# Moving casts, loads and a small reduction at the seam between the decode and the merge stage

## The reference

```
h = rmsnorm(x, g_pre)
z = h @ w_in           # q_lat, kv_lat, k_r, z_att, u_pool, z_pool, g_att, g_pool
...
o_lat = mla_attend(q_abs, q_r, pos, ckv, kr, k_pos)      # prompt: causal blocks; sample: paged cache
o = einsum('bshr,rhv->bshv', o_lat, w_uv)
y_att = (o * silu(z_att)) @ w_o_att
p, pool_state = pool_mixer(u_pool, pool_hist, pos, w_pool, pool_scale)   # windowed means over 2, 4, 8, 16 tokens
y_pool = (p * silu(z_pool)) @ w_o_pool
merged = sigmoid(g_att) * y_att + sigmoid(g_pool) * y_pool
x = x + merged @ w_out                                   # then rmsnorm(x, g_final)
```

## Time and profile before

| | |
|---|---|
| median of 3 runs | 2125.49 us (2124.41 to 2127.14) |
| profiled execution, its own time | 2128.32 us |
| its span, first to last instruction | 2126.5 us (1.8 us lie around it) |
| TensorE busy, matmuls | 2085.4 us, 98% |
| VectorE, ScalarE, GpSimd busy | 1277.5, 972.7, 352.4 us |
| granted TensorE clock, mean | 0.994 of full speed |

### The profile page before, as it was taken

One profiled execution on the slowest core, in us unless ns is written; L12 is line 12 of the kernel. 1 busy time (PEld: TensorE's weight loads), 2 busy tenths in 40 slices (PEclk: granted clock), 3 DMA queues, 4 the chain that ended last, 5 costly groups with the idle time before them and its releaser, 6 DMA issues.

```text
span 2126.5 us, 31437 instructions
## 1 busy us (share of the span) xinstructions
PE 2085.4 (98%) x11893; PEld 1953.7 (92%) x11893; DVE 1277.5 (60%) x2689; ACT 972.7 (46%) x1729; POOL 352.4 (17%) x499
## 2 busy tenths in 40 slices
PE   6999999999999999999999999999999999999997
PEld 6998888888888887799999999999999999999997
DVE  7785878778878775465344644456444644446434
ACT  4445766555555555453334423343334433344333
POOL 3443311011100201150004200050002300041000
PEclk9999999999999999999999999999999999999999
DMA  8876321111110204445434453434534453433532
GB/s 303 251 232 184 92 58 38 45 31 31 31 31 16 100 30 155 152 133 168 136 123 128 141 183 113 145 118 144 165 107 153 131 182 116 128 117 120 178 119 73
DMA packets 159557, 260.44 MB, mean 122 GB/s; under 512 B 21323, under 2 KB 109779, under 8 KB 158247
## 3 DMA queue, kind: packets, MB, share of 16 engines
q1 hardware_dynamic: 153470, 237.59, 35.7%
q0 software_dynamic: 2304, 12.58, 1.6%
q10 hardware_dynamic: 3632, 8.28, 1.3%
HBM read 216.97 MB, written 41.66 MB: 122 GB/s over the span
## 4 chain that ended last, share of the span: by engine, by line
PE 56%; DVE 1%; DMA 0%; ACT 0%; issue 0%; ACTq 0%; POOLq 0%; POOL 0%; DVEq 0%
PE b_ps L122 56%; PE b_ps L2100 1%; DMA d_ws<-in_w 0%; DVE d_y L1988 0%; ACT d_wr L1241 0%; DVE d_y L2008 0%; DVE d_wr L84 0%; DVE d_y L1990 0%; ACT d_y L1889 0%; POOLq L1619 0%; ACT d_zs L1882 0%; ACTq L1619 0%; ACT d_zs L1865 0%; DVE d_gate_p L2016 0%; DVE d_pool L84 0%
## 5 line engine op out<-in xcount | busy, mean ns | idle before, releaser
L122 PE MATMUL b_ps<-d_ht,d_wr 128*128 128x412 f32 x3840 | 734.8, 349 | 1.0 <-DVE d_wr L84 0.7
L122 PEld LDWEIGHTS b_ps<-d_ht,d_wr 128*128 128x128 f32 x3840 | 715.8, 188 | 5.1 <-issue 1.8
L84 DVE TENSOR_TENSOR d_wr<-d_ws,d_wr 128x1024 fp32r<-128x1024 f32 x260 | 321.3, 1236 | 550.7 <-ACT d_wr L1241 550.7
L1241 ACT ACTIVATE d_wr<-d_ws 128x1024 fp32r<-128x1024 f32 x260 | 275.1, 1058 | 600.6 <-PE b_ps L122 591.7
L746 PE MATMUL b_ps<-kt,k_qs 128*128 128x512 f32 (+2 forms) x1520 | 337.3, 370 | 1.6 <-DVE b_p L1090 1.5
L746 PEld LDWEIGHTS b_ps<-kt,k_qs 128*128 128x128 f32 x1520 | 265.7, 188 | 47.5 <-DVE b_p L1090 2.4
L84 DVE TENSOR_TENSOR b_pt<-b_ps,b_pt 128x512 fp32r<-128x512 f32 x272 | 183.5, 689 | 95.4 <-ACT b_pt L1044 93.5
L1044 ACT ACTIVATE b_pt<-b_ps 128x512 fp32r<-128x512 f32 x272 | 158.7, 597 | 174.0 <-PE b_ps L1150 115.3
L1150 PE MATMUL b_ps<-b_pt,kv 128*128 128x512 f32 x816 | 229.6, 410 | 3.6 <-DVE b_pt L84 3.6
L1037 ACT ACTIVATE b_p<-b_p,b_bias 128x1024 f32<-128x1024 f32 (+7 forms) x192 | 171.5, 896 | 54.4 <-DVE b_low L1097 53.4
L122 PE MATMUL b_ps<-d_mrg,d_wr 128*128 128x412 f32 x960 | 189.8, 353 | 0.0
(11 more groups left out here) (212 smaller groups left out, 2066.0 us busy)
## 6 DMA issues: line engine op xcount, KB each, us to landing
d_ws<-in_w SPq DMA_DIRECT2D x260, 512.0 KB, 3.6
out_q<-a_qout SPq DMA_DIRECT2D x32, 384.0 KB, 4.7
d_hf<-out_ht SPq DMA_DIRECT2D x20, 412.0 KB, 3.5
d_olf<-out_olat SPq DMA_DIRECT2D x40, 206.0 KB, 2.9
a_xt<-in_x_t SPq DMA_DIRECT2D x16, 512.0 KB, 5.2
out_ht<-a_hf SPq DMA_DIRECT2D x16, 512.0 KB, 3.7
out_olat<-b_ol SPq DMA_DIRECT2D x32, 256.0 KB, 4.2
out_y<-d_y SPq DMA_DIRECT2D x5, 1536.0 KB
```

Of the source, the lines that this page charges most:

```text
L84: return e.tensor_tensor(low, source, high.bitcast(f32), ALU.subtract)
L122: mm = pe.matmul(out, stationary(a, k), moving(b, k), start=first and k == 0 and a + b == 0, stop=last and k == depth - 1 and a == 1)
L1241: act.activation(ahead["wr"][k % 2][:, 0, :, :], ahead["ws"][k % 4][:, :, :], ACT.Copy).then_inc(ahead["w_hi"], 1)
```

## The change

Four moves. In decode, ScalarE casts the third quarter of the tokens before the first exponentials, not after them. In merge, SyncE issues the loads of weight tiles 4 and 5 ahead of all its other loads; `pscale` and `gfin` are issued from GpSimd's queue, after its clearing of `y`, and no longer from ScalarE's; VectorE reduces the history after tile 1's preparation of weights, not after tile 0's.

```
             for n in range(STEPS):
                 for j in range(QUAD):
                     keys(n, j)
-                    if n == CHUNKS and j == QUAD - 1:
-                        exponents(0)
                 if n in AHEAD_H:
                     h_high(act, ahead, AHEAD_H.index(n) // 2, AHEAD_H.index(n))
+                if n == CHUNKS:
+                    exponents(0)
...
+            for k in range(2):
+                sp.wait_ge(w_ok, k + 1)
+                load_weights(sp, io, ahead, k + 4)
             load_pick(0)
...
-                    if c < NC - 1 or k + 4 < NW:
+                    if (c > 0 or k >= 2) and (c < NC - 1 or k + 4 < NW):
                         after(sp, (w_ok, NW * c + k + 1))
                         load_weights(sp, io, ahead, k + 4)
...
-            act.dma_start(pscale[:, :], io["pool_scale"]).then_inc(const_in, 16)
-            act.dma_start(gfin[:, :], io["g_final"].partition_broadcast(P)).then_inc(const_in, 16)
...
             pool.memset(last[:, :, :], 0.0).then_inc(head_ok, 1)
+            pool.dma_start(pscale[:, :], io["pool_scale"]).then_inc(const_in, 16)
+            pool.dma_start(gfin[:, :], io["g_final"].partition_broadcast(P)).then_inc(const_in, 16)
...
-                    if c == 0 and k == 0:
+                    if c == 0 and k == 1:
                         history()
```

## The result

The changed kernel takes 2128.86 us (median of 20 runs), the kernel before 2125.41 us (20 runs beside them). The ratio is 1.0016, with a 95% interval of 1.0010 to 1.0022: 3.4 us slower, 2.1 to 4.7, and above the range of the prediction. Two executions of the kernel before were far slower (2157.2 and 3301.83 us) and are not in the ratio; its other 18 lie between 2122.61 and 2130.15, wider than the 0.13% of the first three. The profiled execution took 2128.82 us, its span is 2126.9. The two spans differ by only 0.4 us, because decode begins 4.1 us earlier in the second one (827.00 instead of 831.07 us), for reasons outside the change: in every trace but the one of before it begins between 824.5 and 828.1. So I compare stage by stage, from decode's first issue (`c_own`), from merge's first issue, and to the first ZA tile.

A forecast was written before the change was run, and what follows sets the result against it. It took TensorE, busy 98% of the span, as the bound, with 3.3 us idle where the change acts. Decode's -0.6 and merge's +0.8 gave +0.2 on a median of 2125.5: 2125.7 us, range 2123.4 to 2127.7.

The forecast's parts named there:

- Moved cast: In decode: the earlier cast brings VectorE's subtraction, TensorE's turn and the scores forward; 0.6 us gained, bounds +1.4 and -0.4.
- when `wuv_f` lands: At merge's start: behind the loads of tiles 4 and 5, `wuv_f` lands 1.4 us late, between 0.7 and 2.4.
- Who pays: In merge: the lateness passes through ScalarE's square and GpSimd's line to the first ZA tile; 0.8 us lost.
- Edits costed at nothing: In merge: later history and constants on GpSimd's queue stay covered by GpSimd's wait for the square; no cost.
- rival (b): In merge: GpSimd's own issues of the constants decide from 2.2 us each; at 3.5 us each, 2128.3 us; chance 0.08.
- Rival (a): In merge: GpSimd's line is not the end, `wuv_f` landing nearly as before; about 1.3 us gained, 2124.2; chance 0.20.
- Rival (c): In decode: the token quarter lands 0.6 us or more later, nothing gained there; 2126.3 us or a little more; chance 0.14.
- Rival (d): In merge: tile 4's VectorE subtraction waits behind GpSimd's addition for the port; only 0.7 us gained, 2124.8; chance 0.10.
- The sum: Whole kernel: decode's -0.6 us and merge's +0.8 us give +0.2 us, 2125.7 us; chance 0.48.

The follow-up runs named there:

- e5: Changed kernel with `pick`, `wpl_f` and `wuv_f` issued ahead of tiles 4 and 5, which still precede the latents and the history's copy; 2123.45 us, one run.
- e7: Changed kernel with GpSimd's clearing of `y` and the constants' loads behind it held back until `wpl_f` and `wuv_f` have landed; 2133.43 us, one run.
- e8: Changed kernel with `wuv_f` and `wpl_f` split one tile later and TensorE's wait for the split moved to the first pooling product; 2126.74 us, ratio 1.0010.
- e2: Kernel before with only the loads of tiles 4 and 5 issued ahead of SyncE's other loads; 2128.99 us, ratio 1.0016.
- e9: e5 with the history reduced after tile 0 again, as in the kernel before; 2123.42 us, ratio 0.9992.
- e6: Changed kernel with the loads of tiles 4 and 5 issued in decode, behind the second chunk's token quarters; 2124.26 us, ratio 0.9994.
- e1: Kernel before with only the cast of the third token quarter moved ahead of the exponentials; 2125.09 us, ratio 1.0001.
- e3: Changed kernel with SyncE's order of loads put back; moved cast, constants on GpSimd's queue and later history stay; 2123.97 us, ratio 0.9997.
- e11: Changed kernel with `hist` and `head` issued by SyncE behind `wuv_f`, not by ScalarE; 2130.32 us, one run.
- e12: As the changed kernel, but only tile 4's load goes ahead of SyncE's other loads, tile 5's back in its place; 2125.57 us, ratio 1.0001.

## Why the prediction was wrong

**Moved cast: right.** 0.6 was forecast, about 1.0 measured (58.0 to 58.1 against 59.0 to 59.1). Each step came as written: ScalarE's wait for the landing, the cast, the subtraction 0.9 earlier, the copies after the exponentials as the new end. Only the end was 0.35 too late in my sum: four copies take 2.04 in a row, and the scores follow 0.05 later.

**The step that failed: when `wuv_f` lands.** I took 1.4 us late, with bounds of 0.7 to 2.4; it was 5.5. Both of my bounds count the bytes ahead of `wuv_f`, and the near one takes the rate of decode's burst (1848 KB in 7.25 us). Two things differ here. First, merge starts slower than a burst in decode. Windows of the kernel before from the issue of two weight tiles and two token quarters at 870.59, its second to fourth us, and of the changed kernel from merge's start, the same three and the two after them:

```profile
871.59:872.59 1.00, 1.00 (x20) 0.59 (x16) 0.64 (x1) 0.33 (x1) 0.00 (x0) 1.00 0.87 164
872.59:873.59 1.00, 1.00 (x17) 0.61 (x7) 1.00 (x2) 0.00 (x0) 0.00 (x0) 1.00 1.05 410
873.59:874.59 1.00, 1.00 (x12) 1.00 (x11) 0.42 (x5) 0.92 (x2) 0.00 (x0) 1.00 0.98 389
...
886.05:887.05 1.00, 1.00 (x8) 1.00 (x7) 0.00 (x0) 1.00 (x2) 1.00 (x1) 1.00 1.12 86
887.05:888.05 1.00, 1.00 (x7) 0.99 (x6) 0.87 (x1) 0.42 (x2) 1.00 (x1) 1.00 0.75 154
888.05:889.05 1.00, 1.00 (x7) 1.00 (x6) 0.35 (x1) 0.00 (x0) 1.00 (x3) 1.00 0.79 268
889.05:890.05 1.00, 1.00 (x7) 1.00 (x6) 0.00 (x0) 0.18 (x1) 0.93 (x3) 1.00 0.97 388
890.05:891.05 1.00, 1.00 (x7) 1.00 (x6) 0.02 (x1) 0.88 (x1) 0.65 (x1) 1.00 1.02 385
```

In four microseconds (with the first, 4 GB/s in both) decode moves 967 KB, merge 512 KB: 1.2 us at full rate. (The kernel before starts merge no faster, with 391 KB.) This alone would have stayed within my bounds. By 893.05, 8.0 us after merge's start, 2060 KB had moved (the windows' GB/s times us, with 388 and 384 GB/s for the next two), about the 1800 KB and ScalarE's 270 that I had counted for 7.3 to 9.0 us. Second, and this is what failed, `wuv_f` does not end with these bytes. The queues from merge's start to its landing, in the changed kernel (885.05 to 897.17, the first three rows) and in e5 (885.16 to 891.87, the other two): packets, MB, share of 16 engines; q1 is SyncE's, q0 GpSimd's, q10 ScalarE's:

```profile
q1 hardware_dynamic: 1035, 2.58, 70.2%
q0 software_dynamic: 176, 0.53, 12.3%
q10 hardware_dynamic: 288, 0.28, 6.8%
...
q1 hardware_dynamic: 547, 1.25, 66.0%
q10 hardware_dynamic: 288, 0.28, 13.4%
```

SyncE's 1800 KB up to `wuv_f` are 1.84 MB, so 0.74 MB that it issued behind `wuv_f` had moved as well, and all of GpSimd's `gfin`. That is 1.27 MB more than I counted. At the 329 GB/s of the last four microseconds it takes 3.9 us, nearly the way from 8.0 to 12.1. This is accounting after the fact: why `wuv_f` ended behind these bytes no run shows. Nor is it a rule for every load: in e5 only 0.46 MB from behind `wuv_f` (776 KB with what stands ahead, 0.79 MB) had moved, and nothing of `gfin`. For `gfin` it agrees with what I had weighed from the Trainium skill (DMA: Bandwidth & Descriptors, Issuing engines are not separate DMA queues): DMAs of different queues share the same engines and interleave. I applied it to ScalarE's 270 KB only (at the burst's rate 1.06 us, not the 0.7 I wrote), and not to GpSimd's `gfin`; e7, with `gfin` out of the way, landed 2.1 earlier. What SyncE issues behind `wuv_f` on its own queue I did not count at all.

**Who pays: right in kind.** Put 5.5 where the prediction has 1.4. ScalarE's square and GpSimd's norm are then 5.5 late: 9.82 + 5.51 = 15.33 us after merge's start, and 15.33 is what the trace has (900.38). Less the wait of 0.25, GpSimd would end 5.26 later and the ZA tile come at 33.56 + 5.26 + 0.14 = 38.96. GpSimd's operations took 0.53 more than that (it ended at 924.40, after 39.35), and the tile came at 39.64, because TensorE itself was later still: the text said the hole at tile 4 stays closed only under 1.4 of lateness, and at 5.5 it is open by 3.8. What I had no term for is the clock behind such a hole (1.55 us) and the 0.90 at the pooling product. Two paths of nearly equal length were late, and e8, which cuts one, shows the other: 3.39 at the ZA tile.

**Edits costed at nothing.** An issue on GpSimd's queue costs 0.59 and 0.56, near the low end of my bounds; rival (b) is out. The history a step later was covered by the wait for the square in the change (5.51), and with `hist` late it takes a wait off tile 3 (1.03 in e2). As soon as `wuv_f` is in time it is on GpSimd's path: e5 waited 0.75 at the ZA tile, e9 not. Rival (a) needed `wuv_f` as before and did not occur. Rival (c) is out. Rival (d) did not occur at tile 4: VectorE's subtraction started first, at 901.26, and took 1.24, and GpSimd's addition of 901.32 took 1.92 instead of 0.89. It did occur at the pooling operand, where the subtraction of 918.10 took 1.38 instead of 0.57, most of the 0.90 more wait. The Trainium skill (SBUF — State Buffer, Who interferes with whom) has a VectorE instruction with two SBUF inputs contend with a GpSimd instruction that reads SBUF, and both rows agree.

**The sum.** With the measured sizes, -1.0 + 4.9 gives +3.9, and 3.4 was measured (2.1 to 4.7). That it comes so close is in part luck, since it leaves out the clock and the pooling product. The range failed, because both of its bounds stood on the bytes ahead of one load.

## What to carry to other kernels

Where loads are put in another order at the start of a stage, ask for each one that moves back who waits for it first, and price its landing between the end of what stands ahead of it in its own queue and the end of all that every queue issues in that stretch: here 6.4 to 8.0 us where small loads or none stood ahead, 10.0 to 12.8 behind one or two weight tiles. Put the small load with the earliest reader first and the large one with the latest reader last, or into the stage before, if its DMA engines have time (their busy share in decode was 0.28 to 0.29). And when a wait is removed (e8, e6), look for the second path of the same length before counting the gain.

## What the runs showed of the hardware

- The issue of a load can be held for 1.8 to 2.9 us on the issuing engine, not always the same load: `pick` 2.68 (changed), `gfin` on ScalarE 1.79 (e1), `wuv_f` 2.15 (e3) and 2.63 (e6), tiles 4 and 5 together 2.73 (e5), `wpl_f` 2.89 (e7). They all begin 0.9 to 1.4 us after merge's start and end by 4.3, while the transfers are still slow. In e8 and e11 no issue took over 0.8. Neither GpSimd's clearing (e7) nor a second queue (e11) explains the slow start; its cause is open.
- Single DMA packets: the first ones of 2 or 4 KB in merge take some 1.0 to 2.7 us each, in every order, later ones of 4 KB 0.16. When 1 MB of weights goes first (changed), `pick`'s packets of 64 bytes start between 5.4 and 7.6 us after merge's start; when they go first (e9), between 1.0 and 2.3. That the engines' shares run out of step and a load waits for its last share is my reading of this, argued and not shown.
- The granted clock fell to 0.50, the 1.2 GHz level, behind idle stretches of TensorE of 3.25 (e12), 3.39 (e8), 3.52 and 3.39 (e7), 3.81 (changed) and 4.43 us (e11), and stayed at 1.00 behind those of 2.04 (e2) and 2.18 (e3). Where tile 4 followed, it took 6.27 to 6.29 us instead of 4.7.
